# Columns 2 to 7 of the recurrence's branch product as three passes over rounded parts

## The reference, cut to what matters

```
y_a = hgrn2_mixer(...)                      # (L, 512): gated linear recurrence
y_b = dsa_mixer(...)                        # (L, 512): attention over selected keys
merged = sigmoid(gate_a) * (y_a @ w_branch_hgrn) + sigmoid(gate_b) * (y_b @ w_branch_dsa)
h = h + merged @ w_out
h = h + hier_moe(rmsnorm(h), ...)           # 32 experts, then the next layer
```

## Time and profile before

| what | value |
|---|---|
| median of 3 runs | 1759.31 us (1757.56 to 1763.18) |
| profiled execution, first to last instruction (its span; the profile gives it no other time) | 1760.8 us |
| PE matmul busy | 1486.8 us, 84% |
| DVE busy | 708.0 us, 40% |
| ACT busy | 584.1 us, 33% |
| POOL busy | 343.1 us, 19% |
| mean granted TensorE clock | 0.901 |

### The profile page before, as it was taken

The page is one execution under the profiler, slowest core; times in us unless marked ns, Lnnn a source line. Parts: engine busy times, 40 slices in busy tenths (PEclk is TensorE's granted clock), DMA queues, the critical chain, the costliest instruction groups (busy, mean ns, idle before and its releaser), DMA issues.

```text
span 1760.8 us, 30301 instructions
## 1 busy us (share of the span) xinstructions
PE 1486.8 (84%) x11834; PEld 1159.5 (66%) x11834; DVE 708.0 (40%) x1718; ACT 584.1 (33%) x1047; POOL 343.1 (19%) x235
## 2 busy tenths in 40 slices
PE   3999976979999599988579999589899986998882
PEld 3879966977777455554268799588768674555551
DVE  5137987034352411111243399830454324111114
ACT  5234554255422011111243445433554220111112
POOL 4201341220300022222032024113003001222210
PEclk8999986989999599999879899679899986999996
DMA  6111230112253799999632113102024366999994
GB/s 227 49 49 68 83 140 14 61 49 79 84 192 135 281 372 384 387 393 391 242 140 97 49 49 127 68 20 97 18 73 138 133 263 258 383 384 393 393 378 170
DMA packets 91990, 321.95 MB, mean 183 GB/s; under 512 B 15376, under 2 KB 15760, under 8 KB 75232
## 3 DMA queue, kind: packets, MB, share of 16 engines
q1 hardware_dynamic: 75376, 289.46, 43.7%
q0 software_dynamic: 10240, 17.33, 3.0%
q10 hardware_dynamic: 6256, 13.51, 2.1%
HBM read 302.49 MB, written 34.01 MB: 191 GB/s over the span
## 4 chain that ended last, share of the span: by engine, by line
PE 53%; SPq 17%; DVE 15%; issue 6%; DMA 4%; ACT 4%; POOL 0%; ACTq 0%; DVEq 0%; POOLq 0%
PE ps L740 14%; PE ps L763 12%; SPq L558 10%; SPq L564 6%; PE ps L1034 5%; PE ps L750 3%; PE ps L975 3%; DMA r<-w_expert_up 2%; PE ps L1055 2%; DVE sc L1368 2%; PE ps L955 2%; PE ps L983 1%; PE ps L731 1%; PE ps L928 1%; PE ps L1023 1%
## 5 line engine op out<-in xcount | busy, mean ns | idle before, releaser
L763 PE MATMUL ps<-x_high,chunk_high_a 128*128 128x264 f32 x896 | 269.5, 301 | 10.7 <-POOL gate_up_low L2099 7.2
L763 PE MATMUL ps<-x_high,gate_up_low 128*128 128x264 f32 x896 | 265.7, 297 | 0.0
L763 PE MATMUL ps<-x_low,chunk_high_a 128*128 128x264 f32 x896 | 265.7, 297 | 0.0
L2099 POOL TENSOR_TENSOR gate_up_low<-gu_ring,chunk_high_a 128x1024 fp32r<-128x1024 f32 x56 | 135.0, 2423 | 478.3 <-ACT chunk_high_a L1742 478.3
L763 PEld LDWEIGHTS ps<-x_high,chunk_high_a 128*128 128x128 f32 x896 | 180.6, 202 | 14.8 <-issue 14.3
L763 PEld LDWEIGHTS ps<-x_low,chunk_high_a 128*128 128x128 f32 x896 | 180.5, 201 | 0.0
L763 PEld LDWEIGHTS ps<-x_high,gate_up_low 128*128 128x128 f32 x896 | 180.3, 201 | 0.0
L1648 DVE COPY r<-ps 128x512 f32<-128x512 f32 x64 | 44.3, 692 | 303.0 <-PE ps L1023 303.0
L2150 POOL DMA_INDIRECT r<-xrow,idx x64 | 61.4, 960 | 490.8 <-PE ps L1023 260.8
L740 PE MATMUL ps<-gate_up_low,x_high 128*128 128x512 f32 (+1 forms) x352 | 140.5, 399 | 0.0
L2025 ACT ACTIVATE r<-ps 128x256 f32<-128x256 f32 x64 | 24.6, 384 | 314.0 <-PE ps L1034 314.0
(11 more groups left out here) (337 smaller groups left out, 3009.2 us busy)
## 6 DMA issues: line engine op xcount, KB each, us to landing
gu_ring<-w_in SPq DMA_DIRECT2D x20, 2048.0 KB, 9.2
r<-w_expert_down SPq DMA_DIRECT2D x44, 512.0 KB, 19.4
gu_ring<-w_expert_gate SPq DMA_DIRECT2D x20, 1024.0 KB, 19.4
gu_ring<-w_expert_up SPq DMA_DIRECT2D x20, 1024.0 KB, 25.4
dn_ring<-w_expert_down SPq DMA_DIRECT2D x40, 512.0 KB, 18.7
expert<-w_expert_gate SPq DMA_DIRECT2D x12, 1024.0 KB, 17.7
expert<-w_expert_up SPq DMA_DIRECT2D x12, 1024.0 KB, 23.4
expert<-w_expert_down SPq DMA_DIRECT2D x24, 512.0 KB, 19.4
```

Of the source, the lines that this page charges most:

```text
L763: last = mm(o[:, lo:hi], w[:, c, quarter(name, j)], x[:, c, lo:hi], start=c == 0 and k == 0, stop=c == KC - 1 and k == 2)
L2099: G.tensor_tensor(low[:, :, cols], w[:, :, cols], high[:, :, cols].bitcast(F32), ALU.subtract).then_inc(sem["low_p"], 1)
```

## The change

Columns 0 and 1 stay as they are. Columns 2 to 7 are computed like the `wb` columns, in a helper `branch` that both now share. ACT rounds `hq` into `xh` (four copies, counted by `ah_ready`) behind its copies of group 3's transposes, and rounds quarter 1 of the weights there. Quarters 2 and 3 follow behind the copies of group 4's transposes. POOL makes the four remainders of `hq` in `xl` (counted by `al_ready`) and three quarters of remainders of the weights in place. The rounded weights use `high_a`, which the last gate block used, so they wait for `("gb", 3)`; `wo0`, the next user, now waits for `("wa", 7)`.

```
-SPLIT = [..., "hg", "gb0", "wb", "wo0", "wo1"]
-UNITS = {u: n for n, u in enumerate((c, q) for c in SPLIT for q in range(1 if c == "k3" else 4))}
+SPLIT = [..., "hg", "gb0", "wa", "wb", "wo0", "wo1"]
+QUARTERS = {"k3": (0,), "wa": (1, 2, 3)}
+UNITS = {u: n for n, u in enumerate((c, q) for c in SPLIT for q in QUARTERS.get(c, range(4)))}
...
-              **{("wo0", q): ("gb", q) for q in range(4)},
+              **{("wa", q): ("gb", 3) for q in QUARTERS["wa"]},
+              **{("wo0", q): ("wa", 7) for q in range(4)},
...
 # TensorE, fill(n)
-                    pe.wait_ge(*at("ya_ready", 1))
-                    feature_major(("wa", c), ...)
+                    if c // 2 not in QUARTERS["wa"]:
+                        pe.wait_ge(*at("ya_ready", 1))
+                        feature_major(("wa", c), ...)
+                        return
+                    pe.wait_ge(*at("al_ready", HH))
+                    branch("wa", c, xh, xl)
+
+                def branch(name, c, high, low):
+                    _, wh, wl = parts(name)
+                    low_parts(name, c // 2)
+                    take((name, c))
+                    settle(pe)
+                    o = wide((name, c))
+                    for lo, hi in ((0, LT // 2), (LT // 2, LT)):
+                        for j in range(4):
+                            for k, (w, y) in enumerate(((wh, high), (wh, low), (wl, high))):
+                                last = mm(o[:, lo:hi], w[:, j, c * P:(c + 1) * P], y[:, j, lo:hi],
+                                          start=j == 0 and k == 0, stop=j == 3 and k == 2)
+                    last.then_inc(sem["pe_done"], 1)
...
 # ScalarE, behind the copies of the transposes of group n0
+                    if n0 == 3:
+                        act.wait_ge(*at("ya_ready", 1))
+                        done(("gb", 3))
+                        for c in range(HH):
+                            A(xh[:, c, :], hq[:, c, :], ACT.Copy).then_inc(sem["ah_ready"], 1)
+                    if n0 in (3, 4):
+                        for q in ((1,), (2, 3))[n0 - 3]:
+                            high_part("wa", q)
...
 # GpSimd, behind the parts of gb0
+                for c in range(HH):
+                    pool.wait_ge(*at("ah_ready", c + 1))
+                    G.tensor_tensor(xl[:, c, :], hq[:, c, :], xh[:, c, :].bitcast(F32), ALU.subtract).then_inc(sem["al_ready"], 1)
+                for q in QUARTERS["wa"]:
+                    low_part("wa", q)
```

More of the change, by code:

```diff
@@ L61 @@
 CHUNKS = ["k3", "k2", "k1", "hi", "hf", "hq", "ga0", "ga1", "gb1", "hg", "gb0", "wa", "wb", "wo0", "wo1"]
-SPLIT = ["k2", "k3", "k1", "hi", "hf", "hq", "ga0", "ga1", "gb1", "hg", "gb0", "wb", "wo0", "wo1"]
-UNITS = {u: n for n, u in enumerate((c, q) for c in SPLIT for q in range(1 if c == "k3" else 4))}
+SPLIT = ["k2", "k3", "k1", "hi", "hf", "hq", "ga0", "ga1", "gb1", "hg", "gb0", "wa", "wb", "wo0", "wo1"]
+QUARTERS = {"k3": (0,), "wa": (1, 2, 3)}
+UNITS = {u: n for n, u in enumerate((c, q) for c in SPLIT for q in QUARTERS.get(c, range(4)))}
 VSPLIT = ("k3", "k2", "hf", "wo0", "wo1")
@@ L196 @@
     kn_ready=1, rope_i=1, rope_a=1, gs0=48, gs1=48, gs2=32, gs3=64, ga_in0=64, ga_in1=64, gb_in=16, rs_ready=1, e_ready=HH, lnf_ready=HH, k_ready=HH, hk_ready=HH, f_done=HH, rel_used=32, d_ready=STEPS + HP, ex_ready=STEPS + 2 * HP, qe_ready=STEPS,
-    qb_ready=HP, kw_ready=HP, sq_ready=HH, ya_ready=1, mx_ready=40, p_ready=40, pn_ready=40, pt_used=20, mg_ready=8,
+    qb_ready=HP, kw_ready=HP, sq_ready=HH, ya_ready=1, ah_ready=HH, al_ready=HH, mx_ready=40, p_ready=40, pn_ready=40, pt_used=20, mg_ready=8,
     xw0=48, xw1=32, rt_ready=2, rt_exp=2, c_ready=1, ab_ready=1, idx_ready=1, base_ready=1, sct_ready=1, xg_clear=1, am2_ready=1,
@@ L452, in parts @@
         def parts(name):
-            slot, nk, nn = CHUNKS.index(name) % 2, 4 if name == "wb" else KC, {"k3": 40, "wb": 1024}.get(name, 512)
+            slot, nk, nn = CHUNKS.index(name) % 2, 4 if name in ("wa", "wb") else KC, {"k3": 40, "wa": 1024, "wb": 1024}.get(name, 512)
             high = {"k3": high_k3, "k1": high_b, "wb": high_b, "wo1": high_b}.get(name, high_a)
@@ L459, in quarter @@
         def quarter(name, q):
-            n = {"k3": 40, "wb": 2 * P}.get(name, P)
+            n = {"k3": 40, "wa": 2 * P, "wb": 2 * P}.get(name, P)
             return slice(q * n, (q + 1) * n)
@@ L916, in fill @@
                     w = chunk("wa").rearrange("p (c n) -> p c n", c=4)
-                    pe.wait_ge(*at("ya_ready", 1))
-                    feature_major(("wa", c), lambda k: w[:, k, c * P:(c + 1) * P], lambda k, lo, hi: hq[:, k, lo:hi], HH)
+                    if c // 2 not in QUARTERS["wa"]:
+                        pe.wait_ge(*at("ya_ready", 1))
+                        feature_major(("wa", c), lambda k: w[:, k, c * P:(c + 1) * P], lambda k, lo, hi: hq[:, k, lo:hi], HH)
+                        return
[13 more added lines that the diff above has]
+                    last.then_inc(sem["pe_done"], 1)
                 def scores(i, g):
@@ L965, in _ @@
                 pe.wait_ge(*at("yl_ready", 4))
-                _, wh, wl = parts("wb")
                 for c in range(8):
[L968 to L977, removed]
+                    branch("wb", c, yh, yl)
                 def router(i):
```

## The result

| | before | after |
|---|---|---|
| median of 4 runs each | 1760.8 us (1757.56 to 1763.18) | 1774.3 us (1772.24 to 1777.76) |
| ratio | | 1.0076 [1.0057, 1.0095], 13.5 us slower |
| profiled execution: span | 1760.8 us | 1773.8 us |
| mean granted clock | 0.901 | 0.896 |
| PE, DVE, ACT, POOL busy | 1486.8, 708.0, 584.1, 343.1 us | 1492.8, 715.9, 593.6, 368.4 us |

The forecast was +4.4 us; the measured time lies above the whole range. A first sign stands on the page: PE's busy time should have fallen by 8.9 us and rose by 6.0. The first row is the chain's share by engine, the second its share by line; beside the earlier trace rows, DVE, "issue" and ACT have gained a point each, PE has lost three, and POOL stands at 1% for 0%.

A forecast was written before the change was run, and what follows sets the result against it. PE was taken as the bound, with DVE and ACT a few tenths behind. Delays of +3.6 less 0.7 and 0.75 give +2.2 us a layer, +4.4 on the span of 1760.8, so 1763.7 us predicted; range 1756 to 1767.

The forecast's parts named there:

- ACT's copies and roundings: Ahead of ACT's copy of group 3's result: they make group 6's scores 0.7 us late in each layer.
- `normalise` waits for POOL, clock held: DVE's `normalise` between 419 and 429 us stands still until POOL's instructions end: group 6's scores 2.9 us late.
- slow spell of the clock: PE at half clock for 3.4 us after new gaps, 1.7 us a spell; left out of the sum, chance 0.13.
- column 2, group 6: The filler in group 6 ends 0.7 us earlier and the work behind it follows: saves 0.7 us a layer.
- columns 3 and 4, groups 7 and 8: PE already waits there for DVE's branch product, so the shorter fillers save 0.
- column 5, group 9: No scores and no DVE work in the way in group 9: saves 0.75 us a layer.
- columns 6 and 7: Before `wb`: PE saves 1.5 us, then waits for POOL's `yl`; saving 0 to 0.4 us, taken as 0.
- the clock's fall: Rival: gaps at 421, in groups 7 and 8 and before `wb` halve PE's clock: 1767 to 1770.5 us, chance 0.13.
- the lock: In the attention stage, POOL's instructions make DVE's `normalise` stand still: scores +2.9 us, then +3.6 by the next group.
- Group 6's saving of 0.7: In group 6 the shorter filler's 0.7 us a layer was to arrive, the work behind following at once.
- `normalise` passes POOL: Rival: DVE's `normalise` does not wait for POOL, only ACT's +0.7 stands: 1758.1 us, chance 0.22.
- the whole saving arrives: Rival: all 8.9 us of the six columns in two layers reach the end: 1750.4 us, chance 0.07.

The follow-up runs named there:

- without POOL: The changed kernel with POOL's remainders left out, PE using the rounded parts in their place (output not the product): ratio to before 1.0010.
- filled gap: The changed kernel with three extra float32 matmuls, read by nothing, behind group 4's transposes: ratio to before 1.0039.
- passes alone: The changed kernel without ACT's and POOL's preparation, columns 2 to 7 in three passes on other operands: ratio to before 1.0027.
- `yl` first: POOL makes all four remainders of the attention output ahead of `wb`'s second quarter; as the only edit to the kernel before, ratio 0.9991.
- the combination: The changed kernel with remainders on DVE, ACT's copies and quarters spread over groups 3, 4 and 6, and `yl` first: ratio to before 0.9985, again 1.0012.
- the remainders on DVE: The changed kernel with the seven remainders made by DVE behind its branch products instead of by POOL: ratio to before 0.9993.
- the preparation alone: The changed kernel with all of ACT's and POOL's preparation, but the six columns still plain float32 (output not the product): ratio to before 1.0125.

## Why the prediction was wrong, step by step

The stage per layer, each term a difference of two kernels:

| term | from | forecast | measured |
|---|---|---|---|
| ACT's copies and roundings | without POOL - before | +0.7 | +0.63 |
| `normalise` waits for POOL, clock held | filled gap - without POOL | +2.9 | +1.69 |
| slow spell of the clock | after - filled gap | 0 (chance 0.13) | +2.63 |
| column 2, group 6 | passes alone - before | -0.7 | 0 |
| columns 3 and 4, groups 7 and 8 | the same | 0 | 0 |
| column 5, group 9 | the same, 9 to `wb` | -0.75 | -0.54 |
| columns 6 and 7 | the same interval | 0 | 0 |
| sum | | +2.2 | +4.4 |

(Column 5 and columns 6 and 7 lie in one interval; 0.53 to 0.58 us in all profiles of the changed kernel.)

*The step that failed is the clock.* The prediction named the mechanism, its place (the gap of `normalise` at 421), its size in rows and its price, 1.7 us a spell, and then left it out of the sum, with a chance of 0.13, because "the work around the new gaps is denser". It isn't: the gap of 1.47 us stands between transposes and scores whose records add up to 1.66 busy us in 3.4, not far from the 1.06 in 2.50 of the earlier trace rows. The spell came in both layers of all three profiles of the changed kernel, 6.8 us long in five of the six and 3.4 in one, and the long one cost 2.63 us, where two spells of 3.4 us at the forecast's 1.7 would make 3.4; the short one cost 42.71 - 41.67 = 1.04. That it is the gap and not the new matmuls is shown by the filled gap, by POOL's work alone being taken out, and by its move to DVE: each ends the spell in both layers. It makes more than half of the loss in the stage: with the gap filled the kernel measured 1.0039, +6.9 us, nearer the forecast of +4.4; with the clock's fall it was 1.0063 to 1.0076, some +12. That the stage without the clock's part comes near the forecast, 1.8 us a layer for 2.2, is partly luck: the lock was put 1.2 too high and group 6 0.7 too low.

*The lock was right in kind and too large in size.* I had read the earlier trace rows as saying that `normalise` waits, and the durations above show it. Its waits alone cost 1.69 us: 11.36 - 9.92 = 1.44 in the marks of group 6 (filled gap against no POOL), and only 0.27 more by group 7, where I had expected the second pair to cost a further 0.7. With ACT's 0.63 the scores of group 7 were held back 2.3 us and not 3.6; in the changed kernel the clock's fall comes on top.

The Trainium skill ("SBUF — State Buffer", "SBUF: two separate sides") names the shared port of GpSimd and VectorE as one of only two places of contention in SBUF; the stretched `normalise`, 0.90 to 1.72 us for 0.36, agrees with it, also for this kind of instruction, with one input and a factor for each row.

*Group 6's saving of 0.7 was wrong.* I had let the work behind the filler follow it at once, though the earlier trace rows shows the filler itself waiting 0.24 us for DVE: DVE's chain binds this group as it does 7 and 8, where the forecast of 0 held. There the waits of 0.41 and 0.54 us grew to 0.78 and not to the 1.1 and 1.2 of the forecast: the filler also starts 0.1 us later behind the scores, and the transposes ahead of the wait take longer (1.62 for 1.47 in group 7).

*Columns 6 and 7* ended as forecast in a wait for POOL, 1.04 us for some 1.3; with `yl` first it is gone and 1.2 us of their saving arrive. The columns themselves took 2.99 us for 2.92.

*What the sum doesn't hold* is the second step that failed: I had put every stage but this one at nothing. The stages give 8.8 us of 13.0 in the profiled executions, and of the 11.1 to 13.4 that the three ratios make. Some 1.2 more lie between `wb` and the gather (0.1 and 1.3 in the repeats). The rest, up to some 3 us, lies in stages that the change doesn't touch, where two profiles of one kernel already differ by more than that: the first maximum of group 5 stands at 419.61 in one profile of the combination and at 413.25 in the other, with a mean clock of 0.88 and 0.90 ahead of it. Every run has its span and granted clock on record, and span x 2 x (1 - clock) is its time at half speed. Its mean is 370 and 371 us in the two repeats of the changed kernel, 343 and 346 in the runs of the kernel before beside them. Of these 28 and 26 us more, the spells in the stage are 10 to 14, by the profiles. So a further 12 to 18 us at half speed lie elsewhere, in all the runs taken together and not only in a profile. If they cost at most half their length, an estimate, they are enough for what is missing. Without POOL's work the mean is 1 us above before's, with the remainders on DVE 1 below, with the filled gap 8 above, and in the combination 7 and 14 above, which is where its gain can have gone (each difference to within 5 to 9 us). Why these spells fall where they do stays open.

*The rivals.* That `normalise` passes POOL fell with the rows above; that the whole saving arrives fell with the passes alone. The clock's fall is the one that came. Even its 1770.5 us lies below the measured 1774.3, though its stage, +2.2 and one or two spells of 1.7, brackets the +4.4: what it lacked stands outside the stage.

## What to carry to other kernels

Work that goes to an idle engine still has a price where the two engines exclude each other: look which short instructions of the busy engine, on the path to PE, fall into the long ones of the idle engine, and cut or move those. When a change opens a gap in PE's stream, look at the busy time around the gap and not at the gap alone, and price a fall of the clock as likely once it resembles a stretch after which the clock already falls. And before counting a saving on PE, ask of each group whether anything in it already waits for another engine by even a few tenths of a microsecond: in the three such groups here it came to zero.

## What was not expected of the hardware

More matmuls made the stage faster: three that nobody reads, in a gap of 1.47 us, gave back 2.63 us a layer. And a shift in the stage moves what the clock does much later: the combination has a slow spell of 3.4 us some 50 us behind the start of `wb`, in both layers of both its profiles, and so have the kernels with the filled gap and with the preparation alone, while before, after and the rest have none there, on the same work. The start of `wb` being early or late doesn't decide it, since the combination starts it 1.8 us earlier than before and the filled gap 1.8 later; what does, no run settles.
